# One place instead of two beside each block of queries in TensorE's order of work

## The reference, cut to what matters

```
oa: differential attention, 4 heads: softmax(q0 k0) - lam * softmax(q1 k1), two score maps of a head, times v (128 wide)
ob: latent attention (MLA), 8 heads of 64, scores = q_nope k_nope + q_rope k_rope, causal
oc: sliding window (128) attention, 8 heads of 64, keys of two blocks of 128
y = g0 * ((oa * silu(a_z)) @ w_br_a) + g1 * ((ob * silu(b_z)) @ w_br_b) + g2 * ((oc * silu(c_z)) @ w_br_c)
```

## Time and profile before

| | us |
|---|---|
| median of 3 runs | 3075.05 (3071.61 to 3076.36) |
| the profiled execution | 3071.18 |
| its span, first to last instruction | 3069.4 |
| TensorE (PE) matmuls busy | 2972.8 (97%) |
| VectorE busy | 1851.8 (60%) |
| ScalarE busy | 1060.2 (35%) |
| GpSimd busy | 1119.1 (36%) |
| mean granted TensorE clock | 0.986 |

### The profile page before, as it was taken

The page is one execution under the profiler, slowest core; times in us unless marked ns, Lnnn a source line. Parts: engine busy times, 40 slices in busy tenths (PEclk is TensorE's granted clock), DMA queues, the critical chain, the costliest instruction groups (busy, mean ns, idle before and its releaser), DMA issues.

```text
span 3069.4 us, 38687 instructions
## 1 busy us (share of the span) xinstructions
PE 2972.8 (97%) x15272; PEld 2362.1 (77%) x15272; DVE 1851.8 (60%) x3007; ACT 1060.2 (35%) x1875; POOL 1119.1 (36%) x468
## 2 busy tenths in 40 slices
PE   8999999989999999899999999998999999899998
PEld 6777778877777778777777778886788778678886
DVE  4855565565746655645553498714766676588832
ACT  4443443344343432433333322224333333432221
POOL 3322334333223334333333344443333333244442
PEclk9999999999999999999999999999999999999999
DMA  5222222232222223222222223332222222223332
GB/s 192 82 70 70 69 76 96 83 103 69 75 63 69 76 89 97 84 88 83 76 83 76 84 88 98 99 98 79 83 76 76 76 76 76 70 76 97 97 99 71
DMA packets 78328, 260.20 MB, mean 85 GB/s; under 512 B 10730, under 2 KB 13546, under 8 KB 78148
## 3 DMA queue, kind: packets, MB, share of 16 engines
q1 hardware_dynamic: 77572, 255.63, 26.6%
q10 hardware_dynamic: 576, 2.10, 0.2%
HBM read 255.53 MB, written 6.09 MB: 85 GB/s over the span
## 4 chain that ended last, share of the span: by engine, by line
PE 89%; DVE 6%; ACT 2%; DMA 1%; issue 1%; POOL 0%; SPq 0%; ACTq 0%; DVEq 0%
PE bank L671 26%; PE bank L673 25%; PE bank L672 25%; PE bank L786 2%; PE bank L833 2%; PE bank L813 1%; PE bank L991 1%; DVE x_res L1761 1%; PE bank L702 1%; DMA bias_copies<-bias_vectors 1%; PE bank L1027 1%; PE bank L792 1%; PE bank L1065 1%; DVE ret_vt L2111 0%; DMA w_raw<-in_w 0%
## 5 line engine op out<-in xcount | busy, mean ns | idle before, releaser
L538 POOL TENSOR_TENSOR w_lo<-w_raw,w_hi 128x1024 fp32r<-128x1024 f32 x458 | 1115.2, 2436 | 1895.2 <-ACT w_hi L1172 1895.2
L671 PE MATMUL bank<-h_hi,w_hi 128*128 128x512 f32 x2784 | 1124.7, 404 | 43.5 <-DVE h_lo L1749 20.4
L673 PE MATMUL bank<-h_hi,w_lo 128*128 128x512 f32 x2784 | 1092.6, 392 | 0.0
L672 PE MATMUL bank<-h_lo,w_hi 128*128 128x512 f32 x2784 | 1091.3, 392 | 0.0
L1172 ACT CAST w_hi<-w_raw 128x1024 fp32r<-128x1024 f32 x458 | 479.0, 1048 | 1235.6 <-PE bank L673 1217.4
L671 PEld LDWEIGHTS bank<-h_hi,w_hi 128*128 128x128 f32 x2784 | 527.1, 189 | 175.3 <-issue 58.6
L673 PEld LDWEIGHTS bank<-h_hi,w_lo 128*128 128x128 f32 x2784 | 526.0, 189 | 114.9
L672 PEld LDWEIGHTS bank<-h_lo,w_hi 128*128 128x128 f32 x2784 | 527.7, 190 | 100.3
L2026 DVE TENSOR_SCALAR m<-bank,gains 128x512 f32<-128x512 f32 x48 | 36.1, 751 | 309.1 <-ACT ta L1370 185.5
L1303 ACT ACTIVATE probs<-probs,small_columns 128x128 f32<-128x128 f32 (+2 forms) x192 | 101.9, 531 | 175.3 <-DVE small_columns L1804 171.1
L673 PE MATMUL bank<-f_hi,w_lo 128*128 128x512 f32 x352 | 136.9, 389 | 0.0
(11 more groups left out here) (279 smaller groups left out, 3712.1 us busy)
## 6 DMA issues: line engine op xcount, KB each, us to landing
w_raw<-in_w SPq DMA_DIRECT2D x458, 512.0 KB, 3.5
bias_copies<-bias_vectors SPq DMA_DIRECT2D x1, 2560.0 KB
x_res<-in_x_t ACTq DMA_DIRECT2D x4, 512.0 KB, 8.0
bias<-bias_copies SPq DMA_DIRECT2D x8, 256.0 KB, 3.4
bias<-bias_copies SPq DMA_DIRECT2D x16, 128.0 KB, 2.4
out_x<-x_res SPq DMA_DIRECT2D x8, 256.0 KB, 2.0
bias_copies<-bias_vectors SPq DMA_DIRECT2D x1, 1280.0 KB
ple_raw<-in_p_t SPq DMA_DIRECT2D x2, 512.0 KB, 3.8
```

What stands on the lines that cost most here:

```text
L538: pool.tensor_tensor(WL[slot][:], RAW[slot][:], WH[slot][:].bitcast(F32), ALU.subtract).then_inc(sems["lo_done"], 1)
L671: pe.matmul(banks[bank][:], WH[slot][:, w], hi[:, k, :], start=start, stop=False)
L672: pe.matmul(banks[bank][:], WH[slot][:, w], lo[:, k, :], start=False, stop=False)
L673: pe.matmul(banks[bank][:], WL[slot][:, w], hi[:, k, :], start=False, stop=stop).then_inc(sems["kt_done"], 1)
```

## The change

The two places beside a block become one. In the first stack `cuts(n)` gives 5 positions instead of 9: three equal thirds up to `third`, then 4 k-tiles before the end (`BEHIND`), then the end. `third` is the last k-tile but one of the tile that overwrites the queries (q, qn or cq), since the scores of block 3 have to be issued before it is evicted; where there is none it is 8 k-tiles before the end. Worked out: step 0 has its places at k-tiles 17, 24, 31, 36, 40; steps 1, 2 at 8, 15, 23, 36, 40; steps 3 to 6 at 9, 17, 26, 34, 38; steps 7 to 10 at 10, 21, 31, 36, 40; step 11 at 8, 16, 24, 28, 32. Before, a step of 40 had them at 4, 9, 13, 18, 22, 27, 31, 36, 40.

At place i TensorE does scores of block i+1, values of block i-1 and transposes of block i. VectorE's `probs(n, i + 1)` now follows `maxima(n, i + 1)` directly, and so do ScalarE's copies its exponentials. In the dilated pairs the places are at 14, 30, 46 and 60, with the end at 72 as before; VectorE's order is untouched. No instruction of data is added or removed.

```diff
 def cuts(n):
     total = sum(k for _, k in ORDER[n])
     first = PRE if n == 0 else 0
-    share = (total - first) / 9
-    return [upto(n, round(first + share * (p + 1))) for p in range(9)]
+    third = total - 2 * BEHIND
+    for at_, (name, k) in enumerate(ORDER[n]):
+        if name in ("q", "qn", "cq"):
+            third = sum(x for _, x in ORDER[n][:at_ + 1]) - 1
+    share = (third - first) / 3
+    return [upto(n, round(first + share * (p + 1))) for p in range(3)] + [upto(n, total - BEHIND), len(STEPS[n])]
...
# TensorE, first stack
                         for i in range(QT):
-                            fill(n, at_[2 * i])
+                            fill(n, at_[i])
                             if i + 1 < QT:
                                 scores(n, i + 1)
                             if i:
                                 values(n, i - 1)
-                            fill(n, at_[2 * i + 1])
                             turn(n, i)
-                        fill(n, at_[8])
+                        fill(n, at_[4])
...
# TensorE, dilated pairs
                         for i in range(QT):
-                            at_ = 18 * i
-                            first, last = at_ + (6 if i == 3 else 9), at_ + (11 if i == 3 else 18)
-                            steps(nxt, at_, first)
+                            steps(nxt, ((0,) + DIL_PLACES)[i], DIL_PLACES[i])
...
-                            steps(nxt, first, last)
                             t_unit(i, 0)
                             t_unit(i, 1)
-                        steps(nxt, last, 72)
+                        steps(nxt, DIL_PLACES[3], 72)
...
# ScalarE, first stack
                         for i in range(QT):
-                            beside(n, at_[2 * i])
+                            beside(n, at_[i])
                             if i + 1 < QT:
                                 exps(n, i + 1)
-                            beside(n, at_[2 * i + 1])
                             copies_out(n, i)
...
# VectorE, first stack
                         for i in range(QT):
-                            beside(n, at_[2 * i])
+                            beside(n, at_[i])
                             if i + 1 < QT:
                                 maxima(n, i + 1)
-                            beside(n, at_[2 * i + 1])
-                            if i + 1 < QT:
                                 probs(n, i + 1)
```

More of the change, by code:

```diff
@@ L86 @@
 PRE = 10
+BEHIND = 4
 def upto(n, tiles):
@@ L595, in two_stacks_kernel @@
         DAUX, DSCORES, DTURN = 2, 3, 5
+        DIL_PLACES = (14, 30, 46, 60)
         RS0, RTURN = 4, 6
@@ L1340, in mix @@
                                 self.angles_out()
-                        beside(n, at_[8])
+                        beside(n, at_[4])
                         self.step = 0
@@ L1527, in pair @@
                             return
-                        to(9)
+                        to(DIL_PLACES[0])
                         self.v_out(DVT[par][:, 2], DAUX)
                         e_pair(1)
-                        to(18)
                         c_pair(0)
-                        to(27)
+                        to(DIL_PLACES[1])
                         e_pair(2)
                         self.v_out(DVT[nxt][:, 0], DAUX)
-                        to(36)
                         c_pair(1)
-                        to(45)
+                        to(DIL_PLACES[2])
                         e_pair(3)
-                        to(54)
                         c_pair(2)
-                        to(60)
+                        to(DIL_PLACES[3])
                         self.v_out(DVT[nxt][:, 1], DAUX)
-                        to(65)
                         c_pair(3)
```

## The result

The changed kernel is slower: 3082.74 us median (3080.14 to 3085.05, 10 runs) against 3075.09 (3071.33 to 3079.8, 10 runs) in the same comparison, ratio 1.0026, 95% interval 1.0018 to 1.0034. Its profiled execution takes 3083.75 (span 3081.9), 12.6 more than that of before, with a mean clock of 0.983 for 0.986.

The account below looks back on a forecast made before the run. TensorE's own instruction order was taken to bound the kernel. Gross gain 12.0 less 5.2 new waits and 0.5 clock gave 6.3 us less: 3068.7 us median, range 3061.5 to 3079.5.

Parts of the forecast that it names:

- What bounds, and what a merged place saves: TensorE's instruction order is the path; a merged place saves 0.11 us a block, 10.8 us in sum.
- the rival of the hand-over: Longer interval behind scores and values only moves, saving nothing but step 11's stall: 4.5 us more, 3079.5; chance 0.12.
- The new waits that I counted: TensorE waits for qn's bank: 2.4 us at b0 in steps 4 to 6, 2.8 us at z in step 3.
- What comes late next: Block 3's shortened chain between scores and transposes, followed step by step: new waits taken as 5.2 us, bounds zero to 10.
- 6.0 against 5.5: Step 0, block 3: transposes come at 6.0 us, probabilities are there at 5.5, so no wait.
- signs that the prediction named against itself: Waits at L813 of about 2 us, clock falling beside places, or first matmul behind a merged place taking 0.1 back.
- The rival of the lock: VectorE's lock against GpSimd hits block 3's chain, 2.4 us a wait in steps 3 to 6: 3085; chance 0.12.
- The clock: Step 2's column sums now have block 0's place directly behind: 0.5 us added for a fall in layer 0 too.
- that rival: Clock falls in merged places, 1.7 us each: 3080.6 with 7 falls, 3095.9 with 16; chance 0.11.

Follow-up runs that it names:

- the last experiment: Tuned kernel with places chosen by step and angles spread, but dilated pairs as before the change; against the kernel before: 3063.72 us, ratio 0.997.
- the kernel with the three steps alone: One place a block only in steps 0, 1 and 2 of layer 0, all else and pairs as before; against the kernel before: 3086.0 us, ratio 1.0033.

## Why the prediction was wrong

**What bounds, and what a merged place saves: right.** Steps 7 to 10 give 0.37 to 0.43 for 4 x 0.11. A window place after, for the earlier trace rows:

```profile
1031.01 0.66 PE L843 MATMUL bank<-pt,c_v 128*64 128x128 f32 x8
1031.60 0.66 PE L823 MATMUL bank<-ident,probs 128*128 128x128 f32 x4
1032.01 0.48 PE L681 MATMUL bank<-zo_hi,w_hi 128*128 128x512 f32 x1
1032.33 0.39 PE L682 MATMUL bank<-zo_lo,w_hi 128*128 128x512 f32 x1
```

The 0.32 stands once, behind the transposes, and values take the same 0.59 to the next instruction as in the earlier trace rows; the rival of the hand-over falls. Step 11 gave 2.28 where its stalls and places were put at 1.2 + 0.9. The differential steps of layer 1 gave 0.20 and 0.38 for 0.17. The pairs were mis-sized: 0.24 each, 1.7 in all for 2.4. The waits for weights (w_lo) are 9.2 us after and 9.3 before, so the casts at fewer points cost nothing, as forecast.

**The new waits that I counted: right in place and nearly in size.** In step 3 TensorE waits 2.2 in two for the forecast 2.8; yet the two steps together are 3.3 longer, where 2.4 were forecast, and the difference was not followed up. In steps 4 to 6 b0's first matmul starts 0.48 after its predecessor instead of 0.23, and the second 0.33 after that: 0.35 late for the forecast 0.4. Moving the place away gave back 0.4 in each of steps 4 to 6.

```profile
277.17 0.39 PE L683 MATMUL bank<-kvn_hi,w_lo 128*128 128x512 f32 x1
277.65 0.50 PE L681 MATMUL bank<-zo_hi,w_hi 128*128 128x512 f32 x1
277.98 0.39 PE L682 MATMUL bank<-zo_lo,w_hi 128*128 128x512 f32 x1
```

**The step that failed** is in "What comes late next": "for block 3 it has now 13 in steps 1 and 2" k-tiles, after which steps 1 and 2 stand in no term of the new waits (5.2) and so were put at nothing. That counted the k-tiles that the transposes of a block have. For the MLA steps and step 3 it also counted the one eviction queued behind `probs`; for steps 1 and 2 it didn't ask which eviction is queued there, nor what else is. Two facts were to be had from the kernel before and its trace. The place of block 3's scores now stands one k-tile ahead of q's end, and all evictions of the 13 k-tiles that follow it stand behind `probs` in VectorE's order; so q's eviction moves from between `maxima` and `probs` (97.03 in the trace of before) to behind `probs`. And in layer 0 part 2 of the angles follows `probs`, 4.1 us of VectorE from 102.78 to 106.92 in the trace of before. The sum that was made for step 5 of MLA would have read here: probabilities, then 4 instructions of angles, then q's eviction, in front of a tile that wants its bank. The measured price is 9.2 us, with the smaller wait for v, of the same kind, and the clock in it. Moving the angles alone gives 8.9 of it back. In layer 1 the same eviction moves in the same way with no angles in front of it, and step 1 gains 0.38.

**What was not followed either** is block 0 of step 0, where only block 3's chain was added up ("6.0 against 5.5"). VectorE comes late there because it waits for the transfer of the bias, 5.17 us after and 4.75 before:

```profile
44.85 0.69 DVE L1891 TENSOR_TENSOR lat_q<-bank,rstd 128x512 f32<-128x512 f32 x1 [5.17 <-DMA bias<-bias_copies]
```

TensorE then waits twice in the split order (1.1 for the scores' bank, 0.9 for probabilities, 4 k-tiles between them) and once, for 2.8, in the merged one. Over all profiles the merged step 0 is 1.6 to 3.5 longer than that of before, and the split one 0 to 1.6, so a part of the 1.67 is scatter. Two of the signs that the prediction named against itself stand here: a wait for probabilities of about 2 us or more, and a fall of the clock beside a place.

**The rival of the lock** named the mechanism and mis-placed it: the chain of block 3 never lost to it in steps 3 to 6, but q's eviction did. 2.61 and 2.71 for 0.48 and 0.69 are 4.1 us of its delay. No run takes the lock away alone, so its share of the 5.3 us is not measured; in before one instruction of the same part met it (2.51). What the Trainium skill, "SBUF — State Buffer" (Who interferes with whom), says of an exclusive lock agrees with these rows as well as with the earlier trace rows. Its price depends on what stands behind the locked instruction: after the move an instruction of 2.75 beside GpSimd costs TensorE no wait that the trace shows.

**The clock.** 0.5 us was put down, and 7.4 were lost in the three steps. The falls were not in the merged MLA, window or pair places, for which the rival had them: steps 4 to 11 of both layers and the pairs have 1.00 in the windows of the profile after:

```profile
200.00:600.00 400.00, 398.60 (x2059) 1.00 0.27 83
840.00:1240.00 400.00, 399.24 (x2060) 1.00 0.27 82
2124.00:2600.00 476.00, 468.84 (x3303) 1.00 0.26 81
```

The Trainium skill, "TensorE: Matmul & The Clock Gate" (Part 4: PE-mode transpose), had spoken for that rival; with up to eight transposes directly behind other small work, no row here bears it out. Two of the three falls came with stops of TensorE. In step 0 of layer 0 a single wait of 2.6 to 3.8 goes with the low level in all six profiles in which that step is merged. In none of the seven in which it is split, with two waits of 0.9 to 2.4 and k-tiles between, is there a fall. It is worth 1.5 to 2.8. In step 1 it came with the three waits of 4.9 to 5.3 for q, and no other profile has it there. For step 2 I can't say so. A fall behind its column sums came in six of the thirteen profiles, three with merged and three with split places, and a like one in layer 1 in four others. So 3.5 of the 14.4 us in the profile may not be the change's doing. The medians differ by 7.7 and the profiles by 12.6, because the execution profiled before is a fast one of its kernel and the one after is not; falls that come in some executions only could make this scatter, which was not tested.

**What the sum gives.** By stage the profile has 14.4 + 3.3 + 0.5 - 3.3 - 2.3 - 2.5 - 1.7 = 8.4. The two stretches with the falls near 2655 and 2754 add 2.8, and the first 72 k-tiles of the dilated layer 1.2. That one is there also with the pairs unchanged (1.4 in the last experiment) and its cause was not looked for. Some 0.2 of the 12.6 is spread over the rest.

## What to carry to other kernels

When work is regrouped on the busiest engine, write down for every other engine the new order of its queue, with all that stands in it (once-only preparation in one layer too), and ask of each instruction that frees a buffer what now stands in front of it. Work that is late for nobody belongs behind such instructions: here moving 12 of them was worth 8.9 us in their step and 11.3 in the median. Price a stop of TensorE with the clock behind it: one of 5 us cost 2.5 more.

## What the runs showed of the hardware that I had not expected

- A single stop of TensorE in step 0 had a price in clock behind it: 1.5 us behind one of 2.8 (0.62 over 4 us in the profile after), 2.8 behind one of 3.3 in the kernel with the three steps alone (6 x 0.46, its windows):

```profile
51.00:57.00 6.00, 5.96 (x16) 0.54 0.47 164
```

- Behind equal waits, in a stage that the change doesn't touch, a low stretch comes in one profile and not in another: two waits for weights, of 2.50 and 1.85 us, near 2740 had none behind them before, and two of 2.50 and 1.87 had one in the profile after (TensorE's timelines, before and after):

```profile
2741.64 0.47 PE L671 MATMUL bank<-h_hi,w_hi 128*128 128x512 f32 x1 [1.85 <-POOL w_lo L538]
```

```profile
2752.80 0.47 PE L681 MATMUL bank<-h_hi,w_hi 128*128 128x512 f32 x1 [1.87 <-POOL w_lo L546]
```

- VectorE's 128x512 operations of 0.43 to 0.69 us took 2.5 to 2.75 beside GpSimd's subtraction in these rows, with a scalar operand as with two tensors.
